# A decoder trunk: all stacked copies of a conv chunk on ScalarE, and both compression MLPs in one pass on two column halves

## What is computed

```python
u = xn @ w_pw1 + b_pw1                      # conv module: 256 x 2048
a, g = jnp.split(u, 2, axis=-1)
u = a * jax.nn.sigmoid(g)                   # GLU
u = lax.conv_general_dilated(u, w_dw[:, None, :], (1,), padding=[(30, 0)], ...) + b_dw   # 31 taps per channel
u = jax.nn.silu(layer_norm(u, ln_g, ln_b)); return u @ w_pw2 + b_pw2

def compress(x, pe, w1, w2):                # x: T x 4 groups x 64; blocks of 32 tokens, stride 16: 15 blocks
    blocks = (blocks + pe).reshape(B, -1, G, CMP_BLOCK * dh)     # 15 x 4 x 2048
    return jax.nn.gelu(blocks @ w1) @ w2    # 2048 -> 256 -> 64
kc = rope(rms_norm(compress(kv[:, :, 0], cmp_pe[0], cmp_w1[0], cmp_w2[0]), ...))
vc = compress(kv[:, :, 1], cmp_pe[1], cmp_w1[1], cmp_w2[1])
```

## Time and profile before

| | us |
|---|---|
| median of 3 runs | 1385.82 |
| lowest, highest | 1383.53, 1387.02 |
| the profiled execution | 1380.94 |
| its span | 1379.3 |
| TensorE busy in the span | 1047.7 (76%) |
| VectorE busy | 316.2 (23%) |
| ScalarE busy | 289.9 (21%) |
| GpSimd busy | 451.8 (33%) |
| moved | 449.30 MB, 326 GB/s on average |

### The profile page before, as it was taken

The page is one execution under the profiler, slowest core; times in us unless marked ns, Lnnn a source line. Parts: engine busy times, 40 slices in busy tenths (PEclk is TensorE's granted clock), DMA queues, the critical chain, the costliest instruction groups (busy, mean ns, idle before and its releaser), DMA issues.

```text
span 1379.3 us, 27931 instructions
## 1 busy us (share of the span) xinstructions
PE 1047.7 (76%) x10414; PEld 591.1 (43%) x10415; DVE 316.2 (23%) x916; ACT 289.9 (21%) x680; POOL 451.8 (33%) x743
## 2 busy tenths in 40 slices
PE   6958977677677677668999789776676776766668
PEld 5734544333343344334455555443333343333343
DVE  3995300000000000005136852100000000000011
ACT  4643311111111111112112651211111111111111
POOL 3441154433434433430000220553334344362520
PEclk9988989888889888889999899998888898898979
DMA  9942399999999999994315513899999999997930
GB/s 303 358 161 70 123 384 429 429 429 428 430 428 429 429 427 429 429 421 148 128 62 222 206 39 148 324 428 431 427 428 430 427 429 430 427 430 331 429 145 30
DMA packets 62875, 449.30 MB, mean 326 GB/s; under 512 B 10841, under 2 KB 21713, under 8 KB 38256
## 3 DMA queue, kind: packets, MB, share of 16 engines
q1 hardware_dynamic: 57776, 448.25, 78.4%
q10 hardware_dynamic: 5056, 0.48, 0.3%
HBM read 447.66 MB, written 1.05 MB: 325 GB/s over the span
## 4 chain that ended last, share of the span: by engine, by line
DMA 45%; PE 38%; DVE 9%; issue 4%; ACT 2%; SPq 1%; POOL 0%; ACTq 0%; DVEq 0%
DMA ring<-in_moe_w_up 43%; PE PS L554 14%; PE PS L438 9%; PE PS L533 2%; DMA ring<-in_moe_w_down 2%; PE PS L569 2%; DVE hn L1425 1%; DVE arena L1425 1%; PE PS L541 1%; PE PS L426 1%; PE PS L760 1%; PE PS L733 1%; PE PS L576 1%; SPq L317 1%; PE PS L830 1%
## 5 line engine op out<-in xcount | busy, mean ns | idle before, releaser
L554 PE MATMUL PS<-ring,arena 128*32 128x256 f32 x4128 | 341.3, 494 | 210.5 <-DMA ring<-in_moe_w_up 178.7
L554 PEld LDWEIGHTS PS<-ring,arena 128*32 128x32 f32 x4128 | 161.5, 137 | 379.7 <-issue 235.2
L1477 DVE TENSOR_TENSOR arena<-PS,arena 64x256 f32<-64x256 f32 x65 | 27.8, 428 | 635.0 <-ACT arena L1203 629.0
L569 PE MATMUL PS<-ring,arena 128*32 128x256 f32 x2080 | 125.7, 381 | 30.8 <-DVE arena L1480 30.8
L1203 ACT ACTIVATE arena<-PS 64x256 f32<-64x256 f32 x64 | 24.2, 378 | 547.4 <-PE PS L554 547.4
L974 POOL TENSOR_SCALAR arena<-arena 128x32 f32<-128x32 f32 x64 | 18.9, 295 | 338.5 <-PE PS L541 335.5
L933 POOL TENSOR_SCALAR arena<-arena 128x512 f32<-128x512 f32 x67 | 105.7, 1578 | 23.3 <-POOL arena L980 12.9
L569 PEld LDWEIGHTS PS<-ring,arena 128*32 128x32 f32 x2080 | 73.1, 109 | 61.1 <-issue 37.4
L927 POOL TENSOR_SCALAR arena<-arena 128x32 f32<-128x32 f32 x260 | 88.7, 364 | 13.1 <-POOL arena L974 12.9
L935 POOL TENSOR_TENSOR arena<-arena 128x512 f32<-128x512 f32 x67 | 85.4, 1274 | 5.6
L541 PE MATMUL PS<-hn,arena 128*32 128x256 f32 x1072 | 76.6, 399 | 9.8 <-DMA ring<-in_moe_w_down 9.1
(11 more groups left out here) (323 smaller groups left out, 1214.0 us busy)
## 6 DMA issues: line engine op xcount, KB each, us to landing
ring<-in_moe_w_up SPq DMA_DIRECT2D x64, 2048.0 KB, 23.0
ring<-in_moe_w_down SPq DMA_DIRECT2D x64, 2048.0 KB, 24.7
ring<-in_moe_w_gate SPq DMA_DIRECT2D x63, 2048.0 KB, 18.6
wb<-in_ple_w_gate SPq DMA_DIRECT2D x4, 2048.0 KB, 19.6
ring<-in_conv_w_pw SPq DMA_DIRECT2D x3, 2048.0 KB, 19.0
ring<-in_nsa_w_in SPq DMA_DIRECT2D x3, 2048.0 KB, 20.6
wb<-in_nsa_w_in SPq DMA_DIRECT2D x2, 2048.0 KB, 13.6
wb<-in_nsa_cmp_w SPq DMA_DIRECT2D x2, 2048.0 KB, 8.7
```

The costliest lines, as they stand in the source:

```text
L554: i = pe.matmul(PS[32 * j:32 * j + 32, BGU, 0:256].rearrange("q (p c) -> q p c", c=2), xT[:, k, :], w[:, k, :].rearrange("q (p h c) -> q h ...
L569: i = pe.matmul(PS[32 * j:32 * j + 32, BY, 0:Q4], hT[:, c, 32 * f:32 * f + 32], w_dn(s)[:, f, c, Q4 * j:Q4 * (j + 1)], start=(q == 0), sto ...
L1477: return v.tensor_tensor(hh[64:128, :], PS[64:128, BGU, 0:256], gs[64:128, :], ALU.mult)
```

## The change

Three pieces. (1) ScalarE makes all four shifts of a chunk, 16 copies; VectorE's `stack_copies` and its semaphore are gone. (2) The two MLPs' products alternate slice by slice: MLP 0 on the left 64 columns of the array into PSUM partitions 0 to 59, MLP 1 on the right 64 into partitions 64 to 123, both in bank 0; the slices are read 64 wide, so four columns of each belong to the next slice and their results are not used. One `c1_mm` ends both. The gelu is made once over 128 partitions, transposed once (two 128x128 transposes) and copied once (256 values wide). (3) `mlp_out` comes once, behind the query transposes and ahead of the last four key transposes; ScalarE's copy to `h1T` stands behind its query copies. The transfers that waited for `c1_mm` 2 wait for 1.

```diff
@@ SyncE
-            sp.wait_ge(c1_mm, 2)
+            sp.wait_ge(c1_mm, 1)
             sp.dma_start(dense(WB[2]), cols(ple_w_gate[1], 0)).then_inc(ple_in[0], 16)
@@ TensorE
                 pe.wait_ge(xst_act, c + 2)
-                pe.wait_ge(xst_dve, c + 1)
...
-                for j in range(16):
-                    i = pe.matmul(PS[0:60, s, 0:256], Bc[:, s, j, :, :].rearrange("p g n -> p (g n)"), w1[:, j, :], start=(j == 0), stop=(j == 15))
-                i.then_inc(c1_mm, 1)
+            for j in range(16):
+                for s in range(2):
+                    i = pe.matmul(PS[64 * s:64 * s + 64, 0, 0:256], Bc[:, s, 60 * j:60 * j + 64], w1[s][:, j, :], start=(j == 0), stop=(j == 15))
+            i.then_inc(c1_mm, 1)
...
-            def mlp_out(s):
-                pe.wait_ge(c1_g, s + 1)
-                if s == 1:
-                    pe.wait_ge(kc_x, 1)
+            def mlp_out():
+                pe.wait_ge(c1_g, 1)
                 for c in range(2):
-                    i = pe.transpose(PS[:, 0, 256 + 64 * c:256 + 64 * c + 60], h1v[s][0:60, c * P:(c + 1) * P], ident[0:60, 0:60])
+                    i = pe.transpose(PS[:, 1, P * c:P * (c + 1)], h1v[:, c * P:(c + 1) * P], ident[:, :])
                 i.then_inc(c1_t, 1)
...
-            mlp_out(0)
...
+            mlp_out()
             pe.wait_ge(qt_act, 2)
             k_T(2)
             k_T(3)
-            mlp_out(1)
@@ ScalarE
-                for j in range(STACK - 1):
+                for j in range(STACK):
                     for q in range(4):
                         i = nc.scalar.copy(xst[c % 2][32 * j:32 * j + 32, q, :],
...
-            gelu_sigmoid(0)
-            h1T_copy(0)
-            gelu_sigmoid(1)
+            act.wait_ge(c1_x, 1)
+            nc.scalar.activation(sq[:, 512:768], sq[:, 256:512], ACT.Sigmoid, scale=2.0 * float(np.sqrt(2.0 / np.pi))).then_inc(c1_s, 1)
             kT_copy(0, 1)
             kT_copy(1, 2)
...
+            act.wait_ge(c1_t, 1)
+            nc.scalar.copy(h1T, PS[:, 1, 0:256].rearrange("p (c n) -> p c n", c=2)).then_inc(c1_T, 1)
             kT_copy(2, 7)
             kT_copy(3, 8)
-            h1T_copy(1)
@@ VectorE
-            def stack_copies(c):
-                if c >= 2:
-                    dve.wait_ge(tap_mm, c - 1)
-                j = STACK - 1
-                for q in range(4):
-                    i = v.tensor_copy(xst[c % 2][32 * j:32 * j + 32, q, :],
-                                      cv0[32 * q:32 * q + 32, c, DVE_TAPS + j:DVE_TAPS + j + XW])
-                i.then_inc(xst_dve, 1)
...
-            for s in range(2):
-                if s == 1:
-                    dve.wait_ge(c1_g, 1)
-                dve.wait_ge(c1_mm, s + 1)
-                xx, t1, sg = sq[0:60, 0:256], sq[0:60, 256:512], sq[0:60, 512:768]
...
+            dve.wait_ge(c1_mm, 1)
+            xx, t1, sg = sq[:, 0:256], sq[:, 256:512], sq[:, 512:768]
...
```

More of the change, by code:

```diff
@@ L186, in build @@
         peT = carve(32).rearrange("p (s j) -> p s j", s=2)
[L187 removed]
+        h1v = sq[:, 768:1024]
         vcr = carve(256).rearrange("p (g e) -> p g e", g=4)
@@ L753, in _ @@
             q_products(1)
+            w1 = [WB[1 + s].rearrange("p (j n) -> p j n", j=16) for s in range(2)]
             for s in range(2):
@@ L767, in mlp_out @@
+            i.then_inc(c1_mm, 1)
+            def mlp_out():
+                pe.wait_ge(c1_g, 1)
                 for c in range(2):
-                    i = pe.transpose(PS[:, 0, 256 + 64 * c:256 + 64 * c + 60], h1v[s][0:60, c * P:(c + 1) * P], ident[0:60, 0:60])
+                    i = pe.transpose(PS[:, 1, P * c:P * (c + 1)], h1v[:, c * P:(c + 1) * P], ident[:, :])
                 i.then_inc(c1_t, 1)
-                pe.wait_ge(c1_T, s + 1)
-                if s == 0:
-                    for c in range(2):
-                        i = pe.matmul(PS[0:60, 0, 0:64], h1T[:, c, 0:60], w2c[:, 0, c, :], start=(c == 0), stop=(c == 1))
-                else:
-                    for c in range(2):
-                        for g in range(4):
-                            for q in range(4):
-                                i = pe.matmul(PS[32 * q:32 * q + NC_, 1, 256 + 64 * g:256 + 64 * g + 64], h1T[:, c, NC_ * g:NC_ * (g + 1)],
-                                              w2c[:, 1, c, :], start=(c == 0 and g == 0), stop=(c == 1), skip_group_check=True)
+                pe.wait_ge(c1_T, 1)
+                for c in range(2):
+                    i = pe.matmul(PS[0:60, 0, 0:64], h1T[:, c, 0:60], w2c[:, 0, c, :], start=(c == 0), stop=(c == 1))
+                i.then_inc(kc_mm, 1)
+                for c in range(2):
+                    for g in range(4):
+                        for q in range(4):
+                            i = pe.matmul(PS[32 * q:32 * q + NC_, 1, 256 + 64 * g:256 + 64 * g + 64], h1T[:, c, 64 + NC_ * g:64 + NC_ * (g + 1)],
+                                          w2c[:, 1, c, :], start=(c == 0 and g == 0), stop=(c == 1), skip_group_check=True)
```

28 lines of the change are left out of this document (9 added, 19 removed).

## The result

The changed kernel takes 1375.31 us (median of 5 runs, 1369.61 to 1377.72) beside 1385.66 us for the kernel before (5 runs): ratio 0.9917, 95% interval 0.9888 to 0.9946. Measured again on two other occasions it gave 0.9937 (0.9917 to 0.9957) and 0.9942 (0.9923 to 0.9962); by medians the three gains are 10.4, 6.8 and 7.1 us. One disturbed run of 5149 us is left out. The forecast was 7.7 us and 1378.1. The profiled execution took 1377.72 with a span of 1376.0.

What follows compares the result with a forecast made beforehand. Experts' weight streams, started by loads waiting for output projections, were taken to bound the kernel. The convolution's 3.87 us plus attention's 3.8 gave 7.7 us, from 1385.8 to 1378.1, range 1371.5 to 1383.5.

Steps and rivals of the forecast that it cites:

- G1: Start of the GLU on VectorE that begins convolution chunk 1, forecast to move from 34.09 to 35.78 us.
- chunks 1 and 2: Convolution: ScalarE's loop of 7.94 us sets the pace twice, 15.88 us against 17.96 before.
- chunks 3 and 4: Convolution: 21.93 us less VectorE's copies is 18.9; ScalarE's squares waiting for VectorE's pivot add 0.3, giving 19.2.
- chunks 5 and 6: Convolution: 23.97 us becomes 21.53, since chunk 6's 4.32 us stall beside GpSimd's bias additions moves from copies to taps.
- G7: Start of the GLU that begins convolution chunk 7, forecast at 92.39 us against 97.95, 5.56 earlier.
- The start: Convolution: ScalarE's four more copies of chunk 0 stand before chunk 1's GLU, a loss of 1.69 us.
- the stall leaves with the copies: Rival: convolution chunks 5 and 6 take 17.2 us, the convolution gains 8.2, total 1373.8 us; chance 0.12.
- The tail: Convolution's end: chunk 7's four more copies add 1.69 us; TensorE's last taps stay slow at 3.64 us.
- The halves do not overlap: Rival: the MLP pass takes 14 us, attention gains 0.3 and the whole 4.1: 1381.7 us; chance 0.05.
- slower, each change of half pays in full: Rival: the MLP pass takes 24.3 us, attention starts 9.8 late, the kernel is 5.9 slower: 1391.7 us; chance 0.06.
- the clock falls in front of attention: Rival: TensorE's waits lower its clock, doubling some 4 us of first and compressed scores: 1382 us; chance 0.08.
- Passing on: Ending the convolution earlier or starting attention earlier moves all that follows, including the experts' streams, by the same amount.

Runs made afterwards that it cites:

- the convolution alone: The kernel before with only the convolution's edits, ScalarE making all 16 copies: 1378.75 us, ratio 0.9956.
- late additions: The changed kernel with GpSimd's two bias additions to the residual moved from chunk 6 to behind the convolution's last sums: 1371.12 us, ratio 0.9907.
- halves in turn: The changed kernel with all 16 products of the left half first, then all 16 of the right, instead of alternating: 1380.24 us, ratio 0.9976.
- attention's part alone: The changed kernel with the convolution of before, where VectorE makes the fourth shift: 1378.95 us, ratio 0.9969.

## Why the prediction was right, and where its steps missed

The whole came out as forecast, and part of that is luck. The convolution gained 0.9 us more in the profile than the forecast had, and attention's 3.8 us are in none of the three profiles of the changed kernel at L438; that attention adds to the median rests on its part alone (4.1 us by medians) and on the changed kernel's ratios (0.9917, 0.9937 and 0.9942 against 0.9956 for the convolution alone), whose intervals overlap that one's. The convolution's terms, each from the profile, in us:

| stretch | before | forecast | changed |
|---|---|---|---|
| first GLU to G1 | 10.80 | 12.49 | 12.47 |
| chunks 1 and 2 | 17.96 | 15.88 | 15.84 |
| chunks 3 and 4 | 21.93 | 19.2 | 18.07 |
| chunks 5 and 6 | 23.97 | 21.53 | 21.67 |
| G7 to output projection | 16.00 | 17.69 | 17.86 |
| sum | 90.66 | 86.79 | 85.91 |

*The start* costs four more copies, and *chunks 1 and 2* run at ScalarE's pace: both right to 0.04 us. G1 itself stood at 33.81 and not at 35.8, because the first GLU came 1.95 us earlier; in the profiles it lies anywhere from 21.3 to 23.3 us, also with the old convolution (23.29, 23.04 and 22.18), so no part of it is the change's.

*Chunks 3 and 4* were mis-sized by 1.1 us, all of it in chunk 4 (8.49 us; by the forecast's terms 9.6). I took away VectorE's copies and left the taps as they were. But the taps of chunk 4 were stalled before, by the very row that I used as evidence for the pair: 1.27 us at 66.85 beside GpSimd's product of 1.24 at 66.60, and two behind it took 0.94 each beside its sums, together 1.7 more than three taps elsewhere. With the copies gone the two meet elsewhere in the chunk: GpSimd's product at 64.64 takes 2.76 us, the taps run 0.4 apart, and only the sum behind them is stalled (1.08 us at 66.61 instead of 0.42). The difference, 1.74 less 0.66, is the 1.1 us. A stall between two engines that don't wait for each other is a matter of phase, and a change that shifts one of them has to price it anew. The honest term would have been a range, from 0 to 1.7 us.

*Chunks 5 and 6*: the stall landed on the taps as forecast (2.57 and 2.58 us), and the late additions show it to be the pair's. The rival "the stall leaves with the copies" is out. That the sum is right to 0.14 us is chance in part: chunk 5 took 8.15 us where the terms had 8.50, and chunk 6 13.52 where they had 13.03. By the Trainium skill ("SBUF — State Buffer", Who interferes with whom) an instruction of VectorE with two inputs in SBUF and one of GpSimd that reads SBUF exclude each other, and ScalarE has ports of its own. The trace agrees: 4.90 us of additions, two tap instructions of together 5.15 beside them, ScalarE untouched at 6.77.

*The tail* was right, with a last tap group at half clock (3.64 us) as said.

*Attention.* The pass (7.13 against 7.0), the gelu (8.81 behind its start against 8.8) and the wait for h1 (2.16 us against 2) are as forecast. "TensorEngine Tiling (Array Packing)" of the Trainium skill, Key Properties, holds that tiles load and multiply independently; 7.13 against 13.22 us by order alone agrees. "The halves do not overlap" and "slower, each change of half pays in full" are out. The first was also priced too well, at a gain of 0.3 us: with the halves in turn and a pass of 13.22 us the scores start 1.0 us later than before (24.01 against 23.02), part of it by a clock that fell 20.1 us behind the pass's start. At full clock the scores start 18.79 us behind the pass's start where I had 19.2: a gain of 4.2 against 3.8. The term that failed is the clock. I gave "the clock falls in front of attention" 0.08 and a price of some 4 us; it came true in each of the three profiles, and cost up to 1.5 us at the first scores and 3.3 to 5.4 at the second (27.38 and 29.49 against 24.09). At L438 it is 3.3 to 4.5 us (82.51 to 83.76 against 79.22), so the price was right and the chance too low. My argument was that TensorE would be busier between the MLPs and the scores than in the stretch from 770 to 774, where it was slow. I had compared with the worst stretch of before and not with the same stretch of before. From 745 to 750 TensorE was busy 5.00 of 5 us then, still in its pass, and is busy 3.19 of 5 now. From the pass's end to the first scores it was busy 5.90 of 9.0 us before and is busy 5.84 of 11.7 at full clock in attention's part alone: halving the pass takes away work and makes the stretch with waits longer. That this is why the clock falls earlier is likely and not shown.

*Passing on.* From the first GLU to the end of the first experts it is 601.3 us before (601.6 and 601.4 in the other two kernels with the old convolution) and 596.1 to 598.6 in the changed kernel, 596.5 to 597.0 in the four others with its convolution. On average 5.1 us at the output projection (90.8 to 85.7) are 4.5 at the experts' end (601.4 to 596.9), within 1.7 in any one profile: right for this change. The late additions gave 5.1 to 5.6 us more at the first place and only 0.9 to 4.2 at the second. Two things lie between. Up to the load that opens slot 1's stream it is 23.0 us in ten of the fourteen profiles, but 25.1 and 27.2 in the two in which SyncE stood in the wait for the additions. And behind that load it is 487.6 to 489.9 us whatever the kernel. So a gain reaches the stream whole when nothing new stands in SyncE's queue, and 1 or 2 us of it can't be told at the stream's end from one profile. The same holds in layer 1: from L438 to such a load it is 29.08 us in all fourteen, and behind it 530.5 to 534.6.

## What to carry to other kernels

Before a copy is moved from one engine to another, write down the loop of each engine with its durations: the period of the new bound came out to 0.05 us, while every miss was in what the sum left out, a stall between two engines and the clock. When TensorE's work is made shorter between two waits, compare its busy time with the same stretch of before, and give the clock a real chance. When an instruction is moved on an engine, look at who waits for its count, and at what stands behind that wait in a queue: of 5.1 us won on VectorE 2.1 were lost ahead of the experts' stream while SyncE stood 52.1 us in that wait. And an instruction moved out of one stall can make the next: beside the layer norm the same additions cost a product 1.5 us. Before two profiles are compared, see where each lies among the runs of its kernel: here the fastest of one stood against the slowest of the other, and showed 3.3 us of 7 to 10.

## What the runs showed of the hardware

Products that alternate between two halves of 64 columns take 7.13 us for 64 records, and 13.22 in two runs of 32, although each record lasts 381 ns in both. Two additions of 128x1024 on GpSimd (4.90 us) stop VectorE's two-input taps entirely except for one instruction between the two, and ScalarE's copies not at all. Small loads that SyncE issues behind some 6 MB of others take 6.23 and 2.71 us to be issued, and 0.37 and 0.47 where the queue is free. And one and the same program had its clock fall at different points in three executions: 14.1 us behind the start of the pass twice (0.68 and 0.70 in the stretch from 745 to 750 us), and 20.1 us behind it, past 750, in the third.
